# GpSimd sums at full width, half copies on ScalarE, turn tables ahead of the norm: a state-space weight build in a hybrid trunk

## What is computed

```python
h = h + 0.5 * swiglu(rmsnorm(h, ffn1_norm[i]), ffn1_w1[i], ffn1_w3[i], ffn1_w2[i])
hn = rmsnorm(h, mix_norm[i])
m = s5_mixer(...) if i % N_MIXERS == 0 else stick_breaking_mixer(...)
h = h + m
h = h + 0.5 * swiglu(rmsnorm(h, ffn2_norm[i]), ffn2_w1[i], ffn2_w3[i], ffn2_w2[i])
# in s5_mixer, per group g and state p, with abar = exp((re + j im) * dt):
bbar = (abar - 1) / lam * b;  s[t] = abar * s[t-1] + bbar @ u[t];  y[t] = Re(c @ s[t]) + d * u[t]
```

## Time and profile before

| | |
|---|---|
| median of 3 runs | 1111.12 us (1110.93 to 1113.95) |
| profiled execution: its own time | 1109.45 us |
| its span, first to last instruction | 1107.4 us |
| TensorE busy | 1070.8 us, 97% |
| VectorE busy | 779.9 us, 70% |
| ScalarE busy | 589.7 us, 53% |
| GpSimd busy | 275.3 us, 25% |
| mean granted TensorE clock | 0.995 |

### The profile page before, as it was taken

The page is one execution under the profiler, slowest core; times in us unless marked ns, Lnnn a source line. Parts: engine busy times, 40 slices in busy tenths (PEclk is TensorE's granted clock), DMA queues, the critical chain, the costliest instruction groups (busy, mean ns, idle before and its releaser), DMA issues.

```text
span 1107.4 us, 18766 instructions
## 1 busy us (share of the span) xinstructions
PE 1070.8 (97%) x7606; PEld 981.0 (89%) x7606; DVE 779.9 (70%) x893; ACT 589.7 (53%) x796; POOL 275.3 (25%) x279
## 2 busy tenths in 40 slices
PE   6899999989999999999999999999999899999997
PEld 6899999979999888888998888888988888888897
DVE  6788876878757776766687777566455677776666
ACT  6644446642246656554565656454577656565553
POOL 8799998870002000000220000011011100000021
PEclk9999999999999999999999999999999999999999
DMA  8465654432146565656565565656433455656552
GB/s 211 152 190 171 189 171 153 152 106 68 49 143 190 166 197 172 198 184 196 174 190 172 182 200 184 195 187 193 134 115 113 127 179 183 196 185 197 190 182 77
DMA packets 179674, 183.07 MB, mean 165 GB/s; under 512 B 16128, under 2 KB 173456, under 8 KB 179600
## 3 DMA queue, kind: packets, MB, share of 16 engines
q1 hardware_dynamic: 179456, 181.99, 52.7%
q10 hardware_dynamic: 144, 0.04, 0.0%
HBM read 180.95 MB, written 1.05 MB: 164 GB/s over the span
## 4 chain that ended last, share of the span: by engine, by line
PE 69%; DVE 7%; ACT 3%; issue 1%; POOL 0%; POOLq 0%; DVEq 0%; ACTq 0%
PE acc L1791 32%; PE acc L1793 16%; DVE w_lo L984 3%; PE bank L1469 2%; PE bank L1470 2%; PE bank L1471 2%; PE acc L1469 2%; PE acc L1471 2%; PE acc L1470 2%; DVE op_both L997 1%; ACT w_hi L648 1%; PE acc L1601 1%; PE bank L1638 1%; PE stat L1625 1%; PE misc L1601 0%
## 5 line engine op out<-in xcount | busy, mean ns | idle before, releaser
L984 DVE TENSOR_TENSOR w_lo<-raw,w_hi 128x1024 fp32r<-128x1024 f32 x346 | 455.1, 1325 | 198.1 <-ACT w_hi L648 196.3
L648 ACT ACTIVATE w_hi<-raw 128x1024 fp32r<-128x1024 f32 x346 | 356.7, 1040 | 232.4 <-PE acc L1793 89.8
L1791 PE MATMUL acc<-op_both,w_hi 128*128 128x512 f32 x1056 | 370.7, 395 | 1.2 <-DVE op_both L997 0.6
L1793 PE MATMUL acc<-op_both,w_lo 128*128 128x256 f32 x1056 | 296.0, 280 | 0.0
L1791 PEld LDWEIGHTS acc<-op_both,w_hi 128*128 128x128 f32 x1056 | 197.9, 187 | 48.1 <-issue 2.0
L1793 PEld LDWEIGHTS acc<-op_both,w_lo 128*128 128x128 f32 x1056 | 199.6, 189 | 0.0
L1791 PE MATMUL acc<-g_all,w_hi 128*128 128x512 f32 x528 | 183.2, 392 | 0.0
L1469 PE MATMUL bank<-op_both,w_hi 128*128 128x256 f32 x576 | 168.5, 292 | 12.6 <-DVE op_both L997 4.1
L1471 PE MATMUL bank<-op_both,w_hi 128*128 128x256 f32 x576 | 164.3, 285 | 0.0
L1470 PE MATMUL bank<-op_both,w_lo 128*128 128x256 f32 x576 | 164.2, 285 | 0.0
L468 POOL TENSOR_TENSOR square_sum<-squares 128x512 f32<-128x512 f32 x9 | 13.1, 1451 | 584.9 <-issue 579.8
(11 more groups left out here) (319 smaller groups left out, 1634.2 us busy)
## 6 DMA issues: line engine op xcount, KB each, us to landing
raw<-in_ffn_w_dram SPq DMA_DIRECT2D x258, 512.0 KB, 4.2
raw<-in_sb_w_qkv_dram SPq DMA_DIRECT2D x24, 512.0 KB, 3.6
raw<-in_s_w_glu_dram SPq DMA_DIRECT2D x16, 512.0 KB, 3.4
raw<-in_ple_gate_dram SPq DMA_DIRECT2D x16, 512.0 KB, 3.8
raw<-in_s_w_in_dram SPq DMA_DIRECT2D x8, 512.0 KB, 3.4
raw<-in_sb_w_o_dram SPq DMA_DIRECT2D x8, 512.0 KB, 3.4
raw<-in_ffn_w_dram SPq DMA_DIRECT2D x12, 256.0 KB, 3.2
raw<-in_ple_proj_dram SPq DMA_DIRECT2D x4, 512.0 KB, 3.5
```

The costliest lines, as they stand in the source:

```text
L648: act.activation(w_hi[:, slot, 0:width], raw[:, slot, 0:width], ACT.Copy).then_inc(hi_done, 1)
L984: dve.tensor_tensor(w_lo[:, slot, 0:width], raw[:, slot, 0:width], w_hi[:, slot, 0:width].bitcast(F32), ALU.subtract).then_inc(lo_done, 1)
L1791: pe.matmul(pairs[h][:, m].rearrange("p i t -> p (i t)"), wh, x.rearrange("p i t -> p (i t)"), start=first, stop=False, skip_group_check=True)
L1793: return pe.matmul(pairs[h][:, m, 0, :], wl, x[:, 0, :], start=False, stop=last, skip_group_check=True)
```

## The change

Four edits go together. (1) For each part of a table GpSimd makes the two products as before, but combines them in one instruction over all 128 partitions into a new contiguous buffer `dense`, which has two slots and lies where `turn_cos` and `turn_sin` come later. Table i may overwrite its slot when ScalarE has copied table i - 2. (2) ScalarE gets `place_halves(i)`: it waits for table i, and copies each half of 64 partitions, real and imaginary part together (64 x 1024 elements), to its columns. The eight calls stand behind fixed splits, `HALVES_AT` in (g, j). (3) For that ScalarE's groups 1 to 7 are written out where S5 follows, not looped. (4) GpSimd waits for all 16 copies, and then builds the turn tables and `decay` to the end ahead of the norm of S5. TensorE gets a wait for all copies ahead of its first use of the tables.

```diff
--- before.py
+++ after.py
@@ -152,6 +152,7 @@
         turn_cos = sb("turn_cos", [P, NQ, NC])
         turn_sin = sb("turn_sin", [P, NQ, NC])
         decay = sb("decay", [P, NQ, NC])
+        dense = sb("dense", [P, 2, 2, NQ * H], at=spot["turn_cos"])
         within = [sb(f"within{i}", [P, NQ // 2, P], at=half_1[1 - i]) for i in range(2)]
         x_scaled = sb("x_scaled", [P, KD, T], at=half_1[0])
         u_steps = sb("u_steps", [P, NQ, NC], at=spot["g_hi"])
@@ -205,6 +206,7 @@
         angles_ready, phasors_ready = sem("angles_ready"), sem("phasors_ready")
         pool_step = sem("pool_step")
         weights_ready = sem("weights_ready")
+        dense_ready, halves_placed = sem("dense_ready"), sem("halves_placed")
         state_zeroed, state_first = sem("state_zeroed"), sem("state_first")
         turns_ready = sem("turns_ready")
         block_done, block_skip = sem("block_done"), sem("block_skip")
@@ -301,6 +303,8 @@
 
             return 3 if nxt.kind == "s5" else 1
 
+        HALVES_AT = [(1, 6), (2, 4), (3, 2), (3, 5), (4, 4), (5, 2), (5, 5), (6, 4)]
+
         def block_at(c):
 
             i = c - (CHUNKS["ffn1"] - 4 - NQ // 2 + 1)
@@ -573,32 +577,27 @@
                     return x.unsqueeze(2).broadcast_to([P, NQ, n])
                 xy = [tmp[:, i, 0:NQ * H].rearrange("p (q h) -> p q h", h=H) for i in range(2)]
 
-                def both(o, part, j, op):
-                    for e in range(2):
-                        r = slice(64 * e, 64 * e + 64)
-                        tt(o[r, part, :, j, e, :], xy[0][r], xy[1][r], op)
+                def dense_table(i, p_re, p_im, values, signs):
+                    p_re, p_im = over(p_re, H), over(p_im, H)
+                    for part, op in enumerate(signs):
+                        tt(xy[0], p_re, values[:, part])
+                        tt(xy[1], p_im, values[:, 1 - part])
+                        if part == 0 and i >= 2:
+                            pool.wait_ge(halves_placed, 2 * i - 2)
+                        o = dense[:, i % 2, part].rearrange("p (q h) -> p q h", h=H)
+                        pool.tensor_tensor(o, xy[0], xy[1], op).then_inc(dense_ready, 1)
+                        pool.wait_ge(dense_ready, 2 * i + part + 1)
                 for tau in range(TAU):
-                    p_re, p_im = over(f_re[TAU - 1 - tau], H), over(f_im[TAU - 1 - tau], H)
-                    tt(xy[0], p_re, b_in[:, 0])
-                    tt(xy[1], p_im, b_in[:, 1])
-                    both(w_in_state, 0, tau, ALU.subtract)
-                    tt(xy[0], p_re, b_in[:, 1])
-                    tt(xy[1], p_im, b_in[:, 0])
-                    both(w_in_state, 1, tau, ALU.add)
+                    dense_table(tau, f_re[TAU - 1 - tau], f_im[TAU - 1 - tau], b_in, (ALU.subtract, ALU.add))
 
                 pool.wait_ge(state_zeroed, 4)
                 for j in range(1, TAU + 1):
                     if j == TAU:
                         pool.memset(within[0][:, :, :], 0.0).then_inc(weights_ready, 1)
-                    p_re, p_im = over(a_re[j], H), over(a_im[j], H)
-                    tt(xy[0], c_in[:, 0], p_re)
-                    tt(xy[1], c_in[:, 1], p_im)
-                    both(w_state_out, 0, j, ALU.add)
-                    tt(xy[0], c_in[:, 1], p_re)
-                    tt(xy[1], c_in[:, 0], p_im)
-                    both(w_state_out, 1, j, ALU.subtract)
+                    dense_table(TAU + j - 1, a_re[j], a_im[j], c_in, (ALU.add, ALU.subtract))
                 pool.wait_ge(state_first, 4)
                 pool.memset(within[1][:, :, :], 0.0).then_inc(weights_ready, 1)
+                pool.wait_ge(halves_placed, 2 * 2 * TAU)
                 for _ in range(2):
                     tt(sm(mag), sm(mag), sm(mag))
 
@@ -612,20 +611,18 @@
                     xn = [tmp[:, i, 0:NQ * n].rearrange("p (q c) -> p q c", c=n) for i in range(2)]
                     product(turn_cos[:, :, n:2 * n], turn_sin[:, :, n:2 * n], turn_cos[:, :, 0:n], turn_sin[:, :, 0:n],
                             over(cur[0], n), over(cur[1], n), *xn)
-                while n < NC // 2:
+                while n < NC:
                     doubled()
-                    product(*new, *cur, *cur, sm(t0), sm(t1))
+                    if 2 * n < NC:
+                        product(*new, *cur, *cur, sm(t0), sm(t1))
                     cur, new, n = new, cur, 2 * n
-                norm(1)
-                doubled()
                 ts(decay[:, :, :], over(sm(mag), NC), 1.0, 0.0)
                 pool.memset(decay[:, :, 0:1], 0.0).then_inc(turns_ready, 1)
 
             link(pool.memset(w_in_state[:, :, :, :, :, :], 0.0))
             pool.memset(w_state_out[:, 0, 0:NQ // 2], 0.0).then_inc(state_zeroed, 1)
             for st in stages:
-                if st.v != 1:
-                    norm(st.v)
+                norm(st.v)
                 if st.v == 0 and any(o.kind == "s5" for o in stages):
                     s5_parameters()
                 if st.kind == "attn":
@@ -702,6 +699,8 @@
                     split_hi(n + j, m % RING, g * 2 + (m // RING + 1))
                     if nxt.kind == "s5" and isinstance(n, int):
                         s5_blocks(n + j - 3 - n0)
+                        if (g, j) in HALVES_AT:
+                            place_halves(HALVES_AT.index((g, j)))
 
                 def group(g):
                     n = g * 6 + (n0 - 2)
@@ -714,8 +713,12 @@
                     part(n, 6, g)
                     if not isinstance(g, int) or g < NG - 1:
                         part(n, 7, g)
-                with act.Fori(1, NG - peeled(nxt)) as g:
-                    group(g)
+                if nxt.kind == "s5":
+                    for g in range(1, NG - peeled(nxt)):
+                        group(g)
+                else:
+                    with act.Fori(1, NG - peeled(nxt)) as g:
+                        group(g)
                 for g in range(NG - peeled(nxt), NG):
                     group(g)
                 n = n0 + 6 * (NG - 1) - 2
@@ -819,6 +822,14 @@
                     r = slice(64 * e, 64 * e + 64)
                     for part in range(2):
                         act.activation(w_state_out[r, part, :, 0, e, :], c_in[r, part], ACT.Copy).then_inc(state_first, 1)
+
+            def place_halves(i):
+
+                act.wait_ge(dense_ready, 2 * i + 2)
+                for e in range(2):
+                    r = slice(64 * e, 64 * e + 64)
+                    o = w_in_state[r, :, :, i, e, :] if i < TAU else w_state_out[r, :, :, i - TAU + 1, e, :]
+                    act.activation(o, dense[r, i % 2].rearrange("p i (q h) -> p i q h", h=H), ACT.Copy).then_inc(halves_placed, 1)
 
             def s5_phasors():
                 act.wait_ge(angles_ready, 1)
@@ -1566,6 +1577,7 @@
                     if b == 0:
                         pe.wait_ge(state_first, 4)
                     pe.wait_ge(weights_ready, b + 1)
+                    pe.wait_ge(halves_placed, 2 * 2 * TAU)
                     if b:
                         pe.wait_ge(block_first, 8 * b)
                     for k in range(4):
```

## The result

The changed kernel takes 1114.73 us (median of 20 runs, 1111.69 to 1116.15), the kernel before beside it 1109.77 us (20 runs, 1106.26 to 1114.28). The medians lie 5.0 us apart; the ratio is 1.004, with a 95% interval of 1.0029 to 1.005: slower by some 4.4 us. The profiled execution of after took 1112.1 us, its span is 1110.4.

What follows compares the result with a forecast made beforehand. TensorE, busy 97% of the span, was taken as the bound. Stall 6.8 us plus low clock 1.75 less 4.1 saved gave +4.45 us on the profiled 1109.45, 1115.5 us on the median; range 1112.5 to 1121.5.

Steps and rivals of the forecast that it cites:

- Edit 1, a sum of 128 x 512: GpSimd's table build: 1.29 us a sum, 1.6 beside VectorE; some 37 us of GpSimd freed, zero on the end.
- Edit 2, the wait: First copy: ScalarE stands 9.2 us for the table, so TensorE stands 6.8 us (6.2 to 9) for chunk 11.
- The other seven calls: Later copies in ffn1: just in time at tables 1 and 3, early for the rest; claimed to cost nothing.
- The clock: TensorE behind its stall at chunk 11: a stretch of lower clock loses 1.75 us, bounds 1.4 and 3.
- Edit 4: End of ffn1 and norm of S5: VectorE relieved of GpSimd's last doubling, 4.1 us saved, bounds 2.8 and 4.3.
- The 1.0 us near the end of ffn1: TensorE's wait for a `w_lo` there goes once GpSimd is idle beside VectorE: 1.0 us saved.
- The norm's operands: Norm of S5: TensorE's wait of 1.8 us was to stay, GpSimd's sum of squares lying beside them as before.
- Edit 3: ScalarE's ffn1 groups written out: claimed to cost nothing.
- the repeated wait: Rival: slower sums make ScalarE wait again at table 3, and TensorE stand too; about 1120.5 us, chance 0.14.
- the saving was there: Rival judged: the saving near the norm does not come, another wait takes its place; about 1118.8 us, chance 0.10.
- the first table was not in time: Rival judged: first table ready by 49.6 us, copies hide in the slack, only the saving left; 1107.0 us, chance 0.07.
- The faster rival: Copies hide in the slack since the first table is ready in time, leaving -4.1 us; 1107.0 us, chance 0.07.

Runs made afterwards that it cites:

- pe_filled: The changed kernel with TensorE's ffn1 groups written out and 100 matmuls of zeros just ahead of chunk 11; ratio to the kernel before 1.0052.
- norm_between: The changed kernel with the norm of S5 put back between the fifth and the last doubling; ratio to the kernel before 1.0062.
- later_norm_between: The changed kernel with all copies one group of six chunks later and the norm of S5 put back ahead of the last doubling; ratio to before 1.0001.
- turns_first_alone: The kernel before with only the turn tables and decay moved ahead of the norm, weight tables still in halves on GpSimd; ratio to before 1.0061.
- one_group_later: The changed kernel with each of the eight copy calls one group of six chunks later; ratio to the kernel before 1.0006.
- written_out_alone: The kernel before with only ScalarE's ffn1 groups written out instead of looped; ratio to the kernel before 1.000.
- no_wait_places_pieces: The changed kernel with copies at later places, the sixth no longer ahead of its table, and last doubling and decay in four pieces; 1108.13 us, ratio 0.9964.
- later_in_pieces: The changed kernel with all copies one group of six chunks later, and the last doubling and decay cut into four pieces; ratio to before 0.9975.
- spread_in_pieces: The changed kernel with copies at (2,6) to (7,2), the sixth ahead of its table, and last doubling and decay in four pieces; ratio to before 0.9985.

## Why the prediction was right

Forecast 1115.5 us, 4.4 above the median then shown; measured 1114.73, which is 4.4 by the ratio and 5.0 by the medians. The main step, a stall near chunk 11 of 6 to 7 us with a low clock behind it, was right as a mechanism and in its size. The saving in S5 was right too; 1.0 us of the 4.1 was credited to the wrong edit. Step by step:

- **Edit 1, a sum of 128 x 512.** Taken as 1.29 us with VectorE idle: it was 1.29 and 1.26. Beside VectorE I took 1.6; over all sixteen the mean was 1.76, and GpSimd's busy time fell by 32 us, not 37. The first table was ready at 55.2 us, 1.2 earlier than forecast. Two differences lie in that: the products began at 46.83 for 48.83 (1.1 us of it since this execution began earlier, first `r_diag` at 26.60 for 27.71), and their first pair took 3.39 us for 2.53.
- **Edit 2, the wait.** ScalarE stood 8.8 us (forecast 9.2), the copies took 2.13 (2.1), TensorE stood 6.35 (6.8). The other seven calls cost nothing, with one late by 0.75 us at table 3, where the forecast had it 0.3 late.
- **The clock.** The 24 matmuls of chunk 11 begin at 59.96, and the next ones would have begun 2.9 us later at full clock; by the start of group 3, ScalarE's split has slipped from 69.08 to 76.30 us, 7.2, of which the start of chunk 11 (54.55 to 59.96) is 5.4. So 1.8 us for the low clock, forecast 1.75. But in pe_filled, without it, the wait for table 3 came in its place. The size was right, and the notion that it could be saved by itself was not.
- **Edit 4.** Forecast 4.1 us saved. For `r_diag` and `scratch` I had 1.64 + 1.2, and S5 gave 3.0, shown by norm_between to be the place of the last doubling. The 1.0 us near the end of ffn1 came too, but it was booked to the wrong edit: norm_between and later_norm_between have it without edit 4. The norm's operands gave 1.0 more, which I had not expected; this as well comes without edit 4. In the profiles the operands' longest wait is 1.4 to 1.8 us where a `w_lo` wait of about 1.0 us or more lies some 10 us ahead of it, and 0.5 or less where there is none or a shorter one, turns_first_alone apart. So the shorter table build, which I put at zero on the end, is worth 1.3 us in ffn1 in later_norm_between, and edit 4 only the 3.0. In after, of the 2.1 us that went in ffn1, 0.3 came back as a wait for `within`, and some 0.8 in small pieces that I didn't trace. Another step had a hole that the stall hides: "GpSimd goes on ... done at 204.3 ... The norm of S5 finds it free" was right (205.4), but I looked only at who finds GpSimd idle afterwards, and not at who runs beside the wide instructions where they go. one_group_later shows what that costs without the stall: 4.4 us of waits and a fall of the clock. That after pays only the 0.3 us for `within`, which norm_between doesn't have, is luck.
- **Edit 3** costs nothing, as said (written_out_alone).

The sum was 6.8 + 1.75 - 4.1 = +4.45 us; measured in the profile 6.5 (start of chunk 11 behind the first `r_diag`, 33.36 us for 26.84) and 1.8 for the clock, less 1.0 in the rest of ffn1, less 3.0 in S5 = +4.3. The rivals: the repeated wait did not come in after, but was close by, as pe_filled has it; the saving was there; the first table was not in time. The faster rival's price, had its condition been met by moving the calls, would not have been -4.1: one_group_later has +0.7 us by its ratio of 1.0006 and +2.3 by its two stretches.

The Trainium skill (GPSIMD Engine Reference, Key points) says that GpSimd shares its SBUF interfaces with VectorE, and that they contend when the VectorE instruction has two SBUF inputs. The `w_lo` has two, and the trace agrees: 2.93 us beside the last doubling in norm_between, 1.22 without it in after.

## What to carry to other kernels

When a helper engine's result is consumed at a fixed place in another engine's program, compare the two timelines at the first use: an in-order engine that comes 9 us early for a side job holds the main job with it, and a ring of three buffers bridges less than one chunk of that. When work is moved off one critical stretch, price it where it lands: in one_group_later the 3 us saved in S5 cost 6.7 us in ffn1, and cutting the wide instructions into pieces took 4.4 of that off. And a saving on an engine that is 25% busy showed here only through the waits that it took from others.

## What was not expected of the hardware

- How long GpSimd holds VectorE depends on how its work is cut. A `w_lo` (128 x 1024, two SBUF inputs) takes 1.22 us alone, 1.23 to 1.67 beside GpSimd instructions of 256 columns, up to 2.1 to 2.3 beside those of 512, and 3.1 beside those of 1024. The last is 1.9 us more, about what one such GpSimd instruction takes at its shortest (1.92).
- The low clock behind one and the same wait varies. TensorE stands 3.3 us near 30 us in before and in no_wait_places_pieces, and comes back at nearly the same time. In before the matmuls are slow from 34.42 to 37.63 us. In no_wait_places_pieces the granted clock is low from the first matmul on (stretch, length, busy, clock, DMA share, GB/s):

```profile
32.00:34.00 2.00, 1.54 (x7) 0.50 0.68 203
34.00:36.00 2.00, 2.00 (x11) 0.50 0.16 64
36.00:38.00 2.00, 2.00 (x12) 0.50 0.00 0
38.00:40.00 2.00, 2.00 (x17) 0.91 0.11 33
```

- In later_in_pieces and spread_in_pieces the wait near 30 us was 2.7 us, and no low clock followed it. These differences move ffn1: up to chunk 10 it took 22.7 us in spread_in_pieces and 25.1 in no_wait_places_pieces.
- The clock also fell behind shorter waits, and not always behind the same ones. In later_in_pieces TensorE stood 0.99 us at 217.75 and 1.75 at 228.45, and the clock was at 0.50 from 230 to 232 us; in before, waits of 1.07 and 1.44 at nearly the same places brought no fall. In later_norm_between it fell behind waits of 0.46 and 2.25 us, six microseconds apart; in norm_between the same two brought none. What decides it is open.
